# Reordering the mixers in front of an expert layer: projection columns, gated-attention levels and state-space heads in another order, host rows packed

## The chip, the cores and the metric

The kernel runs on one core of a Trainium2 chip. The metric is the device time of one execution in microseconds (us), the median of the runs. All tensors are float32. The engines are named as in the profile: PE (matmul), PEld (weight load), DVE (vector), ACT (scalar), POOL (GpSimd) and SP, whose queue issues the DMAs.

## The reference

One layer of a hybrid backbone over 256 context tokens and 256 latent tokens (D = 1024), then a mixture of experts over the latent tokens. Cut to what matters:

```python
hl = modulate(rmsnorm(xl, norm1_g), mod_l[0], mod_l[1])   # mod = silu(c) @ w_ada + b_ada
hc = modulate(rmsnorm(xc, norm1_g), mod_c[0], mod_c[1])
fl, fc = mixer_inputs(hl), mixer_inputs(hc)               # u = h @ w_in, split in three head groups
#   GLA:   q, k, v, gate, log decays through a low rank (16)      (chunked scan, both directions)
#   RWKV7: token shift of u; r, k, v, decay / a / gate through low ranks (matrix-valued decay)
#   SSD:   4-tap convolution + silu of xs, B, C; dt = softplus; z (8 heads, both directions)
(gla_c, gla_l), (rw_c, rw_l), (ssd_c, ssd_l) = token_mixers(fc, fl)
xl = xl + mod_l[2] * (concat(gla_out, rwkv_out, ssd_out) @ w_out)
hl = modulate(rmsnorm(xl, norm2_g), mod_l[3], mod_l[4])
xl = xl + mod_l[5] * moe(hl)                              # top 4 of 32 experts, clamped SwiGLU, 12 MB of weights each
return rmsnorm(xl, final_norm_g)
```

Context tokens only give the states from which the scans of the latent tokens start.

## The kernel before, in words

Every engine has one list of instructions, written out by hand, that it works off in order; `pe`, `dve`, `act`, `pool` and `sp` are their blocks. PSUM is handed round in four pairs of banks: `round_table()` lists for each product its pair and how many drains it gets. `R.claim` (PE) waits until all earlier products of that pair are drained, `R.filled` and `R.arrived` say that a product stands in it, `R.drained` and `R.emptied` that it has been read out. Nearly every matmul goes through the helper `mm` (L1786).

The stages, in PE's order:

1. Front. SP loads the identity, the tokens and the constants. ACT issues 22 small DMAs of bias, gain and shift rows into `prow`; PE transposes them (L1812, L1813) and DVE copies them into the column table `pc`. SP waits for those rows before it issues the first 8 tiles of `w_ada` (1 MB each, L549), and then 18 small DMAs of small matrices (L560). PE also transposes the latent tokens into `xT` (L1809). `modulation(n)` is one tile of the modulation (8 records of 128x512 on a quarter of the array each); from n = 4 on, filler matmuls stand between (L1798). Then come the normalized and modulated tokens `hT`.
2. Projections. `PROJ` lists 14 products of one or two column tiles of 128, over all 512 tokens or the 256 latent ones, each 8 matmuls deep: B, C, xs0, xs1, z0, z1 (state space), gq, gv, og, lg (GLA), rr, rk, rv, low (RWKV). `W_GROUPS` packs their columns into 7 loads. The other 16 modulation tiles stand between them (`ADA_AFTER`). DVE adds the taps of the convolutions and the token shifts (L1205).
3. Transposes and small sums: the tokens of xs, v, B by token, the log decays summed (`gs`, `gc`, `cc`), the state-space states `st` and scores `sc`.
4. State-space heads. `running_sums(h)` makes the cumulated decays of one head, DVE turns them into exponents (L1300), ACT takes exp (L891, L893), DVE multiplies the weights (L1312, L1320), PE forms the head's output `yp`. The low-rank products of RWKV (`rz`, `ra`, `rg`, `rkn`) and the GLA state `gS` are put between the heads.
5. GLA levels. The attention within 256 tokens is built from nine masked products `l0` to `l8`. For each of the eight levels after the first, POOL makes four exponent arguments (L674 to L677), ACT takes exp (L917), DVE multiplies them with the keys and queries (L1410, signalling `lk_ready`), PE forms two halves `a` and `b` of 8 small matmuls each, and DVE writes them into `att` under a mask (L1118, L1121). Two argument buffers take turns. Reciprocals of the state-space norm and of RWKV's keys (L1388, L1397) and POOL's RWKV preparation (L683 to L696) stand between the levels.
6. GLA output `go`, its norm (L1424), then `gla_done`.
7. RWKV: four tiles in two directions, a chain of small products (`squares`, `series`, ...); its first product `mix_matrices(0)` waits for `scale_by_decays` (L1448 to L1454).
8. Output projection, second norm, routing (L1606 to L1676).
9. Experts: 32 experts of 12 MB, streamed by SP through a ring of eight 2 MB buffers. SP issues the first ones after `cat_ready`, the end of stage 7 (L605).

Of the kernel before, what the change touches and what calls it, by code (L numbers as in the profile page):

```python
# [11 lines left out]
P = 128  # L12
# [55 lines left out]
class Rounds:  # L68
# [36 lines left out]
    def emptied(self, eng, name):  # L105
# [5 lines left out]
PROJ = [  # L111
    ("B", ((SSD0 + 1024, 128, False), (SSD0 + 1152, 128, False))),
    ("C", ((SSD0 + 1280, 128, True), (SSD0 + 1408, 128, True))),
    ("xs0", ((SSD0 + 512, 128, False), (SSD0 + 640, 128, False))),
    ("xs1", ((SSD0 + 768, 128, False), (SSD0 + 896, 128, False))),
    ("z0", ((SSD0, 128, True), (SSD0 + 128, 128, True))),
    ("z1", ((SSD0 + 256, 128, True), (SSD0 + 384, 128, True))),
    ("gq", ((0, 128, True), (128, 128, False))),
    ("gv", ((256, 128, False), (384, 128, False))),
    ("og", ((512, 128, True), (640, 128, True))),  # L120
    ("lg", ((768, 32, False),)),
    ("rr", ((RW0, 128, True), (RW0 + 128, 128, True))),
    ("rk", ((RW0 + 256, 128, False), (RW0 + 384, 128, False))),
    ("rv", ((RW0 + 512, 128, False), (RW0 + 640, 128, False))),
    ("low", ((RW0 + 768, 96, False), (RW0 + 864, 64, True))),
]

W_GROUPS = [(SSD0 + 1024, 512, ("B", "C")), (SSD0 + 512, 512, ("xs0", "xs1")), (SSD0, 512, ("z0", "z1")),
            (0, 512, ("gq", "gv")), (512, 288, ("og", "lg")), (RW0, 512, ("rr", "rk")), (RW0 + 512, 416, ("rv", "low"))]


ADA_AFTER = (1, 1, 1, 1, 2, 1, 1, 0, 2, 1, 2, 1, 1, 1)

RECIP_AT = 3
# [6 lines left out]
def round_table():  # L141
    t = [("x0", 0, 1), ("x1", 1, 1), ("prm", 2, 1), ("ada0", 3, 1), ("mt0", 0, 1)]
    t += [(f"h{i}", i % 2 + 2, 2) for i in range(4)]
    t += [("dtp", 0, 1), ("dt", 1, 1)]
    for i, (n, _) in enumerate(PROJ):
        t += [("gz", 0, 1)] if n == "rk" else []
        t.append((n, (i + 1) % 3, 1))
    for i in (1, 2):
        t += [(f"ada{i}", 3, 1), (f"mt{i}", 3, 1)]

    t += [("xst0", 0, 1), ("xst1", 1, 1), ("gs", 0, 1), ("gk", 1, 1), ("gvt", 0, 1), ("gc", 1, 1), ("Bt", 2, 1), ("cc", 3, 1), ("st", 0, 1), ("sc", 1, 1)]
    for q in range(4):
        t += [(n, g, 1) for n, g in ((("rz0", 1), ("rz1", 1)), (("ra", 0),), (("gS", 1), ("rg", 1)), (("rkn", 0),))[q]]
        t += [(f"dc{2 * q}", 2, 2), (f"dc{2 * q + 1}", 3, 2), (f"yp{q}", q % 2, 1)]
    t += [("sn", 2, 1)]

    for i in range(9):
        t += [(f"l{i}a", (2 * i) % 4, 1), (f"l{i}b", (2 * i + 1) % 4, 1)]
    t += [("rb", 0, 1), ("go", 2, 1), ("gn", 3, 1)]

    t += [("rvt", 1, 1)]
# [76 lines left out]
def hybrid_block(nc, a):  # L238

    with ExitStack() as ctx:  # L240
# [27 lines left out]
        pc = keep.take(162)  # L268
# [4 lines left out]
        dtw, rtw = keep.take(KD, 16), keep.take(KD, E)  # L273
        dtw_and_next = arena[:, dtw_at:dtw_at + KD * 16 + 16]
# [5 lines left out]
        muc, dall, dcol = keep.take(8), keep.take(8), keep.take(4)  # L280
# [22 lines left out]
        prow = sa.take(2, P)  # L303
        diagR = sa.take(4, P)
        sb_ = Area(scratch0, WORDS - 8192 + 4096)
        xtk, Btok = sb_.take(4, 512), sb_.take(2, 256)
# [3 lines left out]
        ea = sb_.take(16)  # L310
        xw = sb_.take(2, 2, 512)
        Sst = sb_.take(2, 512)
        scF, scB = sb_.take(2, 3, P), sb_.take(2, 3, P)
        eD, EI, CI, WD = sb_.take(2, 768), sb_.take(2, 512), sb_.take(2, 512), sb_.take(2, 768)
        ssq = sb_.take(4, L)
        gz = sb_.take(4, 256)
# [219 lines left out]
        def _(sp):  # L536
# [16 lines left out]
            for n in range(8):  # L553
                load_ada(n)
# [2056 lines left out]
```

## Time and profile before

| | us |
|---|---|
| runs shown | 1499.49, 1500.68, 1815.03; median 1500.68 |
| profiled execution | 1503.03, of which the span 1501.1 |
| PE busy | 1336.3 (89%) |
| DVE busy | 411.4 (27%) |
| ACT busy | 227.3 (15%) |
| POOL busy | 53.1 (4%) |
| DMA | 452.44 MB, mean 301 GB/s |
| mean granted TensorE clock | 0.957 of 2.4 GHz |

How to read it: an engine's busy share is an average over nine stages with different limits. Idle time of an engine matters only where it is the engine on which the others wait. The profiled execution is 2.35 us above the median of the runs.

### The profile page before, as it was taken

To read this page: it belongs to the slowest core of one execution; us is meant where nothing else is said; L and a number is where in the kernel's file an instruction comes from. 1 tells how busy PE (TensorE), PEld (TensorE's weight loads), DVE (VectorE), ACT (ScalarE), POOL (GpSimd) and SP (SyncE) were. 2 spreads that over 40 slices of the span, in tenths; PEclk is the share of its full clock that TensorE was granted. 3 is DMA by queue.
4 is the path that set the end of the run, shared out by engine and by line. 5 is a ranking of instruction groups with operands and counts; after the bars stand their busy time and mean duration, and the time that the engine had idled before them with its cause. 6 is when DMAs were issued, how large, how long until landed. Compare 5 with 4: busy or idle time off the path is not lost.

```text
span 1501.1 us, 21678 instructions
## 1 busy us (share of the span) xinstructions
PE 1336.3 (89%) x9148; PEld 639.8 (43%) x9148; DVE 411.4 (27%) x959; ACT 227.3 (15%) x426; POOL 53.1 (4%) x84
## 2 busy tenths in 40 slices
PE   4999998644888979999999999999999999998997
PEld 2545546423878874333333333333333333333332
DVE  0131135487454442112112112112112112111211
ACT  2122103332232131001001001001001001000101
POOL 0000000043121000000000000000000000000000
PEclk8999999866899979999999999999999999999999
DMA  8536510000101197999999999999999999999995
GB/s 331 189 138 226 202 68 0 1 0 19 40 3 59 47 380 290 424 428 426 427 426 428 428 427 428 427 428 427 427 427 429 428 427 427 428 428 426 428 426 234
DMA packets 44886, 452.44 MB, mean 301 GB/s; under 512 B 6998, under 2 KB 10036, under 8 KB 17044
## 3 DMA queue, kind: packets, MB, share of 16 engines
q1 hardware_dynamic: 44544, 451.38, 72.2%
q8 instruction: 53, 0.87, 0.2%
q10 hardware_dynamic: 276, 0.08, 0.0%
q14 instruction: 13, 0.11, 0.0%
HBM read 450.40 MB, written 1.05 MB: 301 GB/s over the span
## 4 chain that ended last, share of the span: by engine, by line
PE 43%; DMA 16%; DVE 3%; issue 1%; ACT 1%; DVEq 0%; SPq 0%
PE PS L1786 42%; DMA arena<-in_moe_w_gu 16%; PE PS L2499 1%; DVE arena L1708 1%; DVE arena L1711 1%; DVE arena L1714 1%; PE PS L2490 1%; ACT arena L1026 0%; DVE arena L1707 0%; DVE arena L1614 0%; ACT arena L1101 0%; DVE arena L1779 0%; ACT L1019 0%; DVEq L240 0%; DVE arena L1643 0%
## 5 line engine op out<-in xcount | busy, mean ns | idle before, releaser
L1786 PE MATMUL PS<-arena 128*64 128x512 f32 (+11 forms) x8746 | 1282.1, 425 | 113.5 <-DVE arena L1410 23.7
L1786 PEld LDWEIGHTS PS<-arena 128*64 128x64 f32 (+7 forms) x8746 | 593.2, 152 | 750.5 <-issue 599.9
L1707 DVE TENSOR_SCALAR arena<-PS 128x256 f32<-128x256 f32 x64 | 38.6, 602 | 522.3 <-PE PS L1786 522.3
L1052 ACT ACTIVATE arena<-arena 128x256 f32<-128x256 f32 x64 | 26.7, 418 | 491.1 <-DVE arena L1707 491.1
L1734 DVE TENSOR_TENSOR arena<-PS,arena 128x512 f32<-128x512 f32 x32 | 22.1, 692 | 219.3 <-PE PS L1786 219.3
L1062 ACT COPY arena<-PS 128x256 f32<-128x256 f32 x32 | 11.9, 373 | 288.7 <-PE PS L2490 288.7
L2499 PE MATMUL PS<-arena 128*128 128x128 f32 x128 | 26.2, 286 | 29.9 <-DVE arena L1714 29.9
L1205 DVE SCALAR_TENSOR_TENSOR arena<-PS,arena 128x255 f32<-128x255 f32 (+5 forms) x68 | 32.7, 481 | 41.8 <-ACT arena L820 39.5
L1708 DVE TENSOR_SCALAR arena<-PS 128x256 f32<-128x256 f32 x64 | 39.0, 610 | 0.0
L2499 PEld LDWEIGHTS PS<-arena 128*128 128x128 f32 x128 | 14.5, 141 | 56.1 <-DVE arena L1714 30.8
L1711 DVE SCALAR_TENSOR_TENSOR arena<-arena 128x256 f32<-128x256 f32 x64 | 27.3, 426 | 2.8
L1714 DVE TENSOR_TENSOR arena<-arena 128x256 f32<-128x256 f32 x64 | 27.3, 426 | 2.2
L1047 ACT COPY arena<-PS 128x512 f32<-128x512 f32 x32 | 18.8, 587 | 46.1 <-PE PS L1786 46.1
L1057 ACT COPY arena<-PS 128x256 f32<-128x256 f32 x64 | 23.5, 368 | 5.6 <-PE PS L2499 5.6
L1477 DVE TENSOR_TENSOR arena<-arena,PS 128x256 f32<-128x256 f32 x40 | 16.9, 421 | 24.4 <-PE PS L1786 23.7
L1690 DVE TENSOR_SCALAR arena<-arena 128x128 f32<-128x128 f32 x64 | 19.1, 341 | 0.0
L1463 DVE COPY arena<-PS 128x512 f32<-128x512 f32 x16 | 11.0, 689 | 27.6 <-PE PS L1786 27.6
L2490 PEld LDWEIGHTS PS<-arena 128*128 128x128 f32 x64 | 6.5, 141 | 24.3 <-issue 24.3
L983 ACT COPY arena<-PS 128x512 f32<-128x512 f32 x16 | 9.4, 587 | 41.3 <-PE PS L1786 41.3
L674 POOL TENSOR_TENSOR arena<-arena 128x128 f32<-128x128 f32 x8 | 3.5, 443 | 320.6 <-DVE arena L1328 309.6
L1300 DVE TENSOR_SCALAR arena<-PS,arena 128x256 f32<-128x256 f32 (+1 forms) x32 | 11.1, 410 | 11.3 <-ACT arena L891 11.2
L2490 PE MATMUL PS<-arena 128*128 128x128 f32 x64 | 14.0, 301 | 0.0
(276 smaller groups left out, 464.0 us busy)
## 6 DMA issues: line engine op xcount, KB each, us to landing
arena<-in_moe_w_gu SPq DMA_DIRECT2D x128, 2048.0 KB, 26.5
arena<-in_moe_w_down SPq DMA_DIRECT2D x64, 2048.0 KB, 29.0
arena<-in_w_ada SPq DMA_DIRECT2D x24, 1024.0 KB, 7.4
arena<-in_w_in SPq DMA_DIRECT2D x5, 2048.0 KB, 9.2
arena<-in_w_out SPq DMA_DIRECT2D x4, 1024.0 KB, 6.7
arena<-in_w_in SPq DMA_DIRECT2D x1, 1664.0 KB, 6.9
arena<-in_consts SPq DMA_DIRECT2D x1, 1536.0 KB, 11.0
arena<-in_w_in SPq DMA_DIRECT2D x1, 1152.0 KB, 5.6
```

The costliest lines, as they stand in the source:

```text
L1052: act.activation(sgm[:, 256 * half:256 * half + 256], glu[:, 256 * half:256 * half + 256], ACT.Sigmoid, scale=ALPHA).then_inc(sig_ready, 1)
L1057: act.copy(actT[:, 2 * half:2 * half + 2].rearrange("p a b c -> p (a b c)"), src).then_inc(actT_ready, 1)
L1205: ins = dve.scalar_tensor_tensor(out=d_, in0=s_, scalar=wgt, in1=d_, op0=ALU.mult, op1=ALU.add)
L1690: ins = dve.tensor_scalar(selw[:, i, :, :], slot_ids.unsqueeze(1).to_broadcast([P, 2, SLOTS]), pos(i), gates[:, i, bass.ds(e, 1)], ALU.is_ ...
L1707: dve.tensor_scalar(by_rest(glu), of_half(0), LIMIT, None, ALU.min).then_inc(glu_ready, 1)
L1708: dve.tensor_scalar(by_rest(lin), of_half(1), LIMIT, -LIMIT, ALU.min, ALU.max).then_inc(moe_vec, 1)
L1711: dve.scalar_tensor_tensor(out=lin[:, cols], in0=lin[:, cols], scalar=1.0, in1=glu[:, cols], op0=ALU.add, op1=ALU.mult).then_inc(moe_vec, 1)
L1714: dve.tensor_tensor(act_[:, cols], lin[:, cols], sgm[:, cols], ALU.mult).then_inc(act_ready, 1)
L1734: dve.tensor_tensor(ye, PS[:, 3, :], m5h, ALU.mult).then_inc(ye_ready, 1)
L1786: ins = pe.matmul(out, lhsT, rhs, start=start, stop=stop, skip_group_check=skip)
L2490: ins = pe.transpose(PS[:, 3, t * P:t * P + P], selw[:, t, :, :].rearrange("p a b -> p (a b)"), ident)
L2499: ins = pe.transpose(dst[:, c * P:c * P + P], act_[:, (2 * half + c) * P:(2 * half + c + 1) * P], ident)
```

## The change

The host lays the inputs out anew: all bias, gain and shift rows as one `params` table (128 x 170), the small matrices as one `mats` table, the tokens, `xT`, `w_ada`, `w_in` and `w_out` so that each load is one contiguous run per partition. The first eight tiles of `w_ada` come as four loads of 2 MB. ACT's row DMAs, the transposes into `prm` and `xT` and three memsets are gone. On SP's queue the order is params, identity, three double tiles of `w_ada`, tokens, the fourth, mats, constants.

The projections come in the order ll, gq, gv, og, B, C, xs0, xs1, z0, z1, rk, rr, sg, rv. `ll` is one tile of 128 columns that holds the RWKV low-rank columns (96) and the GLA ones (32), which were two tiles (`low` and `lg`). GLA's small products stand between gq and B, the levels l0 to l8 from B to rk, each in two halves with half a projection tile (4 matmuls) between them; a level is one PSUM product now, with one drain. PSUM has five groups: the last pair is shared by the modulation products, in bank 7. The state-space heads are formed in four pairs, with `rv`, `rz0`, `rz1`, `ra`, `rkn`, `rg` and `rvt` between. The state-space norm (`sn`) and `rb` go into the RWKV stage. `w_out` isn't held back until `gla_done`.

```diff
-            sp.wait_ge(rows_in, 16 * N_ROWS)
-            for n in range(8):
-                load_ada(n)
...
+            sp.dma_start(prm, a["params"]).then_inc(params_in, 16)
+            sp.dma_start(Cb(C_ID), a["consts"][:, 0:P]).then_inc(ident_in, 16)
+            for n in (0, 2, 4):
+                load_ada(n)
+            sp.dma_start(xtok, a["tokens"]).then_inc(x_in, 16)
+            load_ada(6)
+            sp.dma_start(mats, a["mats"]).then_inc(mats_in, 16)
...
+    t += [("ll", 0, 2), ("gq", 1, 1), ("gz", 2, 1), ("gv", 0, 1), ("gk", 2, 1), ("gs", 3, 1), ("og", 1, 1), ("gvt", 2, 1), ("gc", 3, 1)]
+    t += [("B", 0, 1), ("C", 1, 1), ("ada1", 4, 1), ("mt1", 4, 1), ("xs0", 0, 1), ("xs1", 1, 1), ("gS", 3, 1), ("z0", 0, 1), ("z1", 1, 1)]
+    t += [(f"l{i}", 2, 1) for i in range(9)]
...
@@ tensor
+            project_in("B", 1, early)
+            level(0, 1)
+            project_in("B", 1, late)
+            project_in("C", 0)
+            project_in("C", 1)
+            modulation_columns(1)
+            level(1, 0)
+            project_in("xs0", 0, early)
+            level(1, 1)
+            project_in("xs0", 0, late)
+            level(2, 0)
...
+            project_in("sg", 0)
...
+            running_sums(0)
+            pe.wait_ge(xw_ready, 4)
+            R.emptied(pe, "Bt")
+            R.claim(pe, "st")
...
+            project_in("rv", 0)
+            decay_logits(0)
+            running_sums(1)
+            R.emptied(pe, "st")
+            head_pair(0)
+            project_in("rv", 1)
+            decay_logits(1)
+            running_sums(2)
+            head_pair(1)
...
+            running_sums(3)
+            head_pair(2)
...
+            values_by_token("rvt")
+            head_pair(3)
@@ vector
+            level_out(dve, 1)
+            level_keys(2)
+            level_out(dve, 2)
+            level_keys(3)
+            convolve(2, "xs0")
+            level_out(dve, 3)
+            level_keys(4)
...
+            for q in range(4):
+                if q:
+                    dve.wait_ge(w_ready, 2 * q)
+                exponents(2 * q)
+                exponents(2 * q + 1)
+                if q:
+                    gather_heads(q - 1)
+                weights(2 * q)
+                weights(2 * q + 1)
...
+                if q == 1:
+                    shift("rv", 4, (vT[:, 0, :], P, NT), (vT[:, 1, :], P, NT))
...
+            dve.wait_ge(kk_std, 1)
+            for c in range(2):
+                dve.reciprocal(kk[:, c, :], kk[:, c, :]).then_inc(kk_norm, 1)
+            gather_heads(3)
...
@@ vector, RWKV stage
+                    if s == 0 and j == 0:
+                        ssd_scale()
+                    if s == 0 and j == 2:
+                        ssd_norm()
```

## Rows read from the trace of the kernel before

**Rows 1.** Busy time by stretch: stretch and its length, each engine's busy time, PEclk, DMA share, GB/s
```profile
19.98:39.67 19.69, 16.35 (x95) 6.04 (x95) 1.22 (x6) 3.40 (x6) 0.00 (x0) 0.74 0.94 377
56.35:226.80 170.45, 168.22 (x573) 84.81 (x573) 42.40 (x87) 23.11 (x30) 0.00 (x0) 0.98 0.41 149
226.80:241.16 14.36, 9.76 (x83) 9.01 (x79) 7.00 (x16) 7.49 (x11) 0.00 (x0) 0.91 0.00 1
241.16:320.00 78.84, 57.64 (x236) 37.99 (x236) 43.99 (x103) 26.40 (x31) 6.42 (x10) 0.85 0.00 1
320.00:355.00 35.00, 9.61 (x132) 7.29 (x128) 33.23 (x33) 5.99 (x9) 23.67 (x31) 0.55 0.00 1
355.00:372.96 17.96, 10.73 (x44) 6.19 (x44) 8.82 (x13) 5.97 (x10) 0.00 (x0) 0.88 0.03 3
372.96:521.00 148.04, 128.88 (x3322) 118.56 (x3323) 71.82 (x168) 35.64 (x80) 21.51 (x35) 0.94 0.09 33
565.80:1501.00 935.20, 881.83 (x4352) 322.07 (x4352) 174.94 (x448) 96.87 (x213) 0.00 (x0) 1.00 0.98 414
```
**Rows 2.** Timeline of the front: start, length, engine, line, operation [idle before, releaser]
```profile
14.86 4.09 SPq L549 DMA_DIRECT2D arena<-in_w_ada  x8
...
19.98 1.94 PE L1786 MATMUL PS<-arena 128*32 128x512 f32 x8 [4.73 <-DMA arena<-in_w_ada]
...
29.86 1.93 PE L1786 MATMUL PS<-arena 128*32 128x512 f32 x8 [0.56 <-DMA arena<-in_w_ada]
...
39.73 0.69 DVE L1161 COPY arena<-PS 128x512 f32<-128x512 f32 x1 [15.20 <-PE PS L1786]
```
**Rows 3.** PE's groups by form, 61.5 to 226.8 us: records, busy, mean ns of one
```profile
L1786 PE MATMUL PS<-arena 128*128 128x512 f32 x201 | 87.9, 595 | 0.0
L1786 PE MATMUL PS<-arena 128*128 128x256 f32 x176 | 41.2, 394 | 0.0
L1786 PE MATMUL PS<-arena 128*32 128x512 f32 x144 | 23.3, 601 | 2.2 <-DMA arena<-in_w_ada 2.2
```
**Rows 4.** DVE's groups by form, 56 to 373 us
```profile
L1121 DVE COPY_PREDICATED arena<-arena,PS 128x512 f32<-128x512 int32 x14 | 9.5, 730 | 0.1
...
L1300 DVE TENSOR_SCALAR arena<-PS,arena 128x256 f32<-128x256 f32 x16 | 7.6, 478 | 11.3 <-ACT arena L891 11.2
L1397 DVE RECIPROCAL arena<-arena 128x512 f32<-128x512 f32 x2 | 6.7, 3336 | 0.0
...
L1351 DVE TENSOR_TENSOR arena<-arena 128x1024 f32<-128x1024 f32 x1 | 1.2, 1226 | 0.0
```
**Rows 5.** ACT's and POOL's groups by form, up to 373 us
```profile
L891 ACT ACT_TABLE_LOAD x2 | 2.6, 1283 | 0.0
...
L690 POOL TENSOR_TENSOR arena<-arena 128x1024 f32<-128x1024 f32 x1 | 2.4, 2352 | 0.0
```
**Rows 6.** Timeline of DVE: the taps of one convolution; one tile of a shift
```profile
96.57 6.17 DVE L1205 SCALAR_TENSOR_TENSOR arena<-PS,arena 128x254 f32<-128x254 f32 x12 [12.30 <-ACT arena L820]
...
214.28 0.75 DVE L1251 TENSOR_SCALAR arena<-PS,arena 128x512 f32<-128x512 f32 x1 [9.25 <-PE PS L1786]
215.06 2.04 DVE L1205 SCALAR_TENSOR_TENSOR arena<-PS,arena 128x255 f32<-128x255 f32 x4
```
**Rows 7.** Timeline of the GLA levels
```profile
329.12 2.52 POOL L687 TENSOR_TENSOR arena<-arena 128x1024 f32<-128x1024 f32 x1
329.47 2.72 DVE L1410 TENSOR_TENSOR arena<-arena 128x512 f32<-128x512 f32 x1
...
336.61 0.63 DVE L1410 TENSOR_TENSOR arena<-arena 128x512 f32<-128x512 f32 x1
...
337.29 1.26 PE L1786 MATMUL PS<-arena 32*128 32x128 f32 x16 [3.79 <-DVE arena L1410]
```
**Rows 8.** Timeline of the first RWKV products
```profile
372.96 1.13 PE L1786 MATMUL PS<-arena 64*64 64x64 f32 x32 [4.83 <-DVE arena L1454]
...
383.13 0.69 DVE L1463 COPY arena<-PS 128x512 f32<-128x512 f32 x1 [5.04 <-PE PS L1786]
```

More of the change, by code:

```diff
@@ L485, in Cb @@
             return C[:, i:i + n, :].rearrange("p a b -> p (a b)")
[L488 removed]
+        loads = [(s, 2, "ada", 2 * m) for m, s in enumerate((0, 2, 4, 12))]
         def streamed(kind, n):
@@ L509, in hybrid_block @@
                 holder[q] = (s, base[s])
+        for n in range(0, 8, 2):
+            place["ada", n + 1] = place["ada", n]
         def w_in_tile(n):
@@ new lines, in _ @@
+            dve.wait_ge(gn_std, 1)
+            run(dve.reciprocal(gsq, gsq))
+            for q in range(2):
+                step(dve.scalar_tensor_tensor(out=gO[:, q, :], in0=gO[:, q, :], scalar=B(72 + q), in1=gsq[:, q, :], op0=ALU.mult, op1=ALU.mult))
+            settle()
+            R.emptied(dve, "og")
+            dve.tensor_tensor(cat[:, 0:2, :], gO, gog, ALU.mult).then_inc(gla_done, 1)
+            shift("rr", 0, (rT[:, 0, :], P, L), (rT[:, 1, :], P, L))
+            shift("sg", 7, (sgT, 64, L))
@@ L1432, in _, with ssd_scale, ssd_norm @@
+            def ssd_scale():
+                dve.wait_ge(sn_std, 1)
+                run(dve.reciprocal(s2[:, 0:512], s2[:, 512:1024]))
+            def ssd_norm():
+                for q in range(4):
+                    step(dve.scalar_tensor_tensor(out=cat[:, 4 + q, :], in0=cat[:, 4 + q, :], scalar=B(68 + q),
+                                                  in1=s2[:, q // 2 * 256:q // 2 * 256 + 256], op0=ALU.mult, op1=ALU.mult))
             dve.wait_ge(rw_pre, 1)
@@ L1949, in _ @@
             R.filled("gc", ins)
-            modulation_columns(2)
+            project_in("B", 0)
+            level(0, 0)
+            project_in("B", 1, early)
[9 more added lines that the diff above has]
+            level(2, 0)
+            project_in("xs0", 1, early)
+            level(2, 1)
+            project_in("xs0", 1, late)
+            level(3, 0)
+            project_in("xs1", 0, early)
+            level(3, 1)
+            project_in("xs1", 0, late)
+            level(4, 0)
+            project_in("xs1", 1, early)
+            level(4, 1)
+            project_in("xs1", 1, late)
+            level(5, 0)
+            pe.wait_ge(gkw_ready, 1)
+            R.emptied(pe, "gvt")
+            R.claim(pe, "gS")
+            for d in range(2):
+                for t in range(2):
+                    ins = mm(pair("gS")[:, 256 * d:256 * d + 256], gkw[:, t, P * d:P * d + P], gvk[:, t, :], start=t == 0, stop=t == 1)
+            R.filled("gS", ins)
+            level(5, 1)
+            project_in("z0", 0)
+            project_in("z0", 1)
+            level(6, 0)
+            project_in("z1", 0)
+            level(6, 1)
+            project_in("z1", 1)
+            level(7, 0)
+            pe.wait_ge(conv_silu, 2)
             R.claim(pe, "Bt")
@@ L1955, in _ @@
             R.filled("Bt", ins)
+            level(7, 1)
+            R.claim(pe, "sc")
+            for g in range(2):
+                for t in range(2):
+                    ins = mm(pair("sc")[:, 512 * g + 256 * t:512 * g + 256 * t + 256], BT[:, g, L + t * P:L + t * P + P], CT[:, g, :])
+            R.filled("sc", ins)
+            project_in("rk", 0, early)
+            level(8, 0)
+            project_in("rk", 0, late)
+            level(8, 1)
             pe.wait_ge(dt_ready, 1)
```

983 lines of the change are left out of this document (470 added, 513 removed).

## The prediction, made before the changed kernel was run

> **What bounds the kernel now.** I read the busy time by stretch first, because 89% busy PE hides stages with different limits. The experts fill 935 us: PE is busy for 882 us of it and the DMA queues for 98%, at 414 GB/s [rows 1]. Their first load waits for the end of the RWKV stage, and neither their bytes nor their code change, so this stretch moves as a block and the question is only how much earlier it starts. In the projections PE is busy for 168.2 of 170.5 us at full clock, so PE alone bounds them; DVE works a quarter of that time [rows 1]. From 241 to 320 us, the state-space heads, no engine is full: PE 57.6, DVE 44.0, ACT 26.4 of 78.8 us. From 320 to 355 us, the levels, PE does 9.6 us of work in 35 us, at a mean clock of 0.55, behind a DVE that is busy for 33.2 us. Until 373 us the GLA norm adds 18 us with PE 60% busy. So 146 us between the projections and the first RWKV product hold only about 88 us of PE work, part of it at the low clock, while 128 us of DVE time lie idle under the projections. That is the reserve that the change draws on.
>
> **The change part by part.** All times are in the profiled execution (span 1501.1, with its surroundings 1503.0), 2.35 us above the median.
>
> *Front.* Now the first modulation tile starts at 19.98 us, because SP issues it at 14.86, after the rows; the tiles then land one per 2.5 us (19.98 and 29.86 are four tiles apart), and the eighth one's product is read at 39.73 [rows 2]. The new queue carries 10.7 MB up to the last of the eight tiles: 0.15 for params and identity, 8.4 for the tiles, 2.1 for the tokens. At 2.5 us per MB (1.05 MB a tile, 420 GB/s) this is 25.5 us, and with 2.6 us from issue to flow (5.1 us from 14.86 to 19.98 less one tile) the last lands at 28 to 29. Two tiles of 1 to 1.9 us and one row of fillers later the product is read at about 32.7: 7 us gained. Bounds: 2 us, if the mix of sizes flows at the 377 GB/s of the stretch and PE comes back to its low clock [rows 1], and 10 us.
>
> *One tile fewer.* A full tile is 16 records of 128x512, 87.9/201 = 0.437 us each, so 7.0 us, half of that for a latent tile [rows 3]. `ll` saves one: 7.0 us, PE-bound time, no unknown. The transposes into `xT` and `prm` lay in the DMA wait and save nothing more. Fifteen full tiles become fourteen.
>
> *From the first projection to the last before rv.* Twelve full tiles 83, twelve half tiles 41, 16 modulation tiles (23.3 us less the 6.9 of lg, over 16: about 1.05) 17, gz, gk, gs, gvt, gc, gS, Bt, sc, cc, go, gn, xst and the modulation's transposes about 21 (their records at 0.11 us per 128 columns at the full clock), nine levels of 0.8 (1.26 at a low clock [rows 7], 0.63 were it all at the full one) 7: 169 us of PE work. Is a level ready when PE comes to it? Between two levels PE has at least 7 us of projection. A level needs four small POOL operations (1.9 us), an exp, one DVE multiply of 0.63 and a masked copy of 1.35 [rows 4, 7]; the convolution of a pair of tiles, 6.2 us [rows 6], comes in between three times, each after the key product that the next level needs. DVE's sum per full tile is 2.0 plus 3.1, of 7.0 us. I follow the queues level by level and find one stall, 0.5 us, where the modulation row is copied after B's convolution. Then `st` cannot be claimed until DVE has shifted `sg`, behind a reciprocal of 3.35 [rows 4], the GLA product and the shift of rr: PE has run 170 us and waits till 177 after its start, with one running sum to fill it. Sum 177 us. Zero stalls is the lower bound; the upper one is 20 us, eight levels that each wait 2.5 us for a chain such as now costs PE 3.79 us [rows 7].
>
> *Heads.* After st (3.4 us) DVE is the engine to follow. Its work in 241 to 320 was 44.0 us [rows 1]; about 9.5 of that (scores, GLA keys and state, gate, squares, norm, last gather) goes elsewhere, and the shift of rv comes in, two tiles of 0.75 and 2.04 [rows 6]: 40 us. Waits that stay: the rz1 product behind rv, and before the last pair ACT's three sigmoids with two table loads of 1.28 [rows 5], 6 us together. With st 3.4 that is 49 us. The same DVE work took 60 us in the old lock step, in which each head's exponents waited for ACT (11.3 us [rows 4]); in pairs, the second head's exponents cover the first one's exp.
>
> *From the last weights to the first RWKV product.* Two reciprocals 6.7 [rows 4]; POOL's two products 2.35 each [rows 5] and DVE's two of 1.23 [rows 4] in the same time; ssd variance 0.7 and the first scaling 1.7. DVE's multiply took 2.72 instead of 0.63 us when it began inside a POOL operation and ended with it [rows 7], so the four products run one after the other: 7.2. Sum 16.5 us. POOL's preparation of RWKV's keys, three operations of about 2.4, now lies beside the last heads instead of the levels. The row shows one DVE operation held for 2.1 us, so I allow 3 us for all of it. The Trainium skill (SBUF — State Buffer, "SBUF: two separate sides") states more and speaks against the change: DVE, with two SBUF inputs, and POOL exclude each other for a whole instruction, and the loser blocks. By that rule all 7 us of the preparation could be lost to DVE and the sum would be 4 us longer; the row agrees in kind.
>
> *RWKV stage.* It gains the norm's reciprocal (3.35) between the first squares' copy, at 383.13 [rows 8], and the series that PE waits for, 2 us of four scalings, and `rb` (1 us) in the chain at its end: 5 us, bounds 2 and 9. `w_out` and `xT` load earlier, in idle DMA time, and cost nothing; were that cover gone, 5.2 MB at 414 GB/s would be 13 us, but the output projection is 130 us away.
>
> *The sum.* From the start of the projections to the RWKV product: 177 + 49 + 16.5 = 242.5, against 372.96 - 56.35 = 316.6: 74 us less (the saved tile is in it). The front gives 7, the RWKV stage takes 5, POOL's lock and some thirty hand-overs of about 0.1 us take 6. 74 + 7 - 5 - 6 = 70: 1503 - 70 = 1433, and 1431 as a median.
>
> **The clock** is the second place. PE at 0.55 in the levels and 1.00 in the projections [rows 1] means that the same 128x512 record costs 0.87 or 0.44 us. In the levels PE had waited about 4 us before each burst; under the projections it has no such wait, so I price all of it at 2.4 GHz. The Trainium skill (TensorE: Matmul & The Clock Gate, Part 1) says that the half clock is the default and that activity releases it. By that rule too the result hangs on PE having no holes, and holes would turn it round: that is the slower rival.
>
> **Rivals.**
> - *The lock step stays* (17%). Each queue works in order, so a level can stand behind a convolution and a head behind the rv shift. Against it: DVE has 28% of slack under the projections. For it: `st` waits for `sg` already. Price: the heads at their old pace, 60 + 6 + 3.4 for 49, is +20, and eight levels that wait 1.3 us each, +10: 1461.
> - *Only the front and the tile pay* (8%). With so many products in few PSUM groups, some thirty claims could each wait 2 us for a drain on a DVE with 5 us operations in front. Then 60 us are given back and the result is 1491, within 2%. The present projections claim in the same way and wait 2.2 us in all [rows 3], which speaks against it.
> - *PE falls to 1.2 GHz in the projections* (4%), slower. Place: the 155 us of projection and modulation matmuls, where each level is now a point at which PE may wait. Price: all of them at 1.2 GHz is +155, 1586; it decides from 100 us on, two thirds of that stretch. Against it: 0.98 in this stretch, with the DMA wait of 2.2 us inside [rows 1, 3].
> - *The packed rows do nothing* (in the front's bound): the bytes are the same, and if these and not the issue at 14.86 set the end, the front gives 2 and the total 1436.
>
> **How the numbers follow.** Main case 71%: 1431, own range 1415 to 1450 (front 5, RWKV 4, no stalls and no lock -6 below; 8 for the lock, 10 for stalls above). The range of 8 in 10 takes in the lock step and ends at 1464. A measurement can tell about 2% from no change, 30 us here: faster than 1471 in the first two cases, 0.88; within 2%, 0.08; slower 0.04.
>
> **What would show it.** In the profile after: the first modulation product at 8 to 10 us; `ll` starting near 49; PE near 100% and PEclk 1.0 from there to about 220, no idle before a level over 1 us, an idle of up to 4 us before st; the heads' four pairs 8 to 14 us apart, DVE over 80% busy; the first 64x64 product of RWKV at 292 to 299; the experts' stretch unchanged at 935 us, 70 us earlier. Wrong would be: PE waiting at levels for DVE, a clock under 0.9 in the projections, or experts that end less early than they begin.

## The result and the profile after

The changed kernel takes 1436.56 us (median of four runs, 1436.17 to 1439.66), the one before 1502.78 in the same series: ratio 0.9577, 95% interval 0.9556 to 0.9597, so 4.2% faster. One of the four executions of the kernel before, 1815.03 us, was a slow one and stands outside the ratio; the three others have a median of 1500.68. The forecast was 1431, range 1414 to 1464. The profiled execution has a span of 1434.4 us against 1501.1. Below, stages are compared between profiled executions, one for each kernel.

Busy time by stretch after the change, columns as in [rows 1]: stretch and its length, PE, weight loads, DVE, ACT, POOL, PEclk, DMA share, GB/s.

```profile
29.52:35.46 5.94, 5.94 (x27) 2.75 (x28) 1.05 (x5) 0.90 (x2) 0.00 (x0) 0.55 1.03 432
50.54:235.78 185.24, 180.33 (x813) 101.78 (x813) 71.95 (x141) 44.71 (x58) 13.81 (x32) 1.00 0.38 138
235.78:289.93 54.15, 48.34 (x197) 29.70 (x197) 41.63 (x90) 19.59 (x24) 7.65 (x4) 0.95 0.11 39
289.93:310.45 20.52, 11.15 (x40) 7.91 (x41) 16.89 (x16) 5.08 (x10) 9.44 (x5) 0.73 0.00 1
310.45:454.00 143.55, 127.91 (x3318) 116.47 (x3319) 75.97 (x171) 37.01 (x81) 21.29 (x34) 0.95 0.05 18
499.00:1434.40 935.40, 881.71 (x4352) 321.80 (x4352) 175.66 (x450) 96.86 (x213) 0.00 (x0) 1.00 0.98 414
```

The levels' stretch at clock 0.55 is gone. The projections, now with the levels inside, have PE busy for 97% at full clock. (PEclk 1.00 is 2.4 GHz, 0.50 is 1.2 GHz.) The experts take 935.4 us as before. In the heads PE is now busier than DVE (48.3 against 41.6 of 54.2 us).

The timeline of the changed kernel, PE, then DVE from the heads on. The end of a line names the idle time before it and what ended it.

```profile
10.10 3.64 PE L1782 MATMUL PS<-arena 128*32 128x512 f32 x16 [10.10 <-DMA arena<-in_ada_first]
...
29.52 1.93 PE L1782 MATMUL PS<-arena 128*32 128x512 f32 x8 [3.41 <-DMA arena<-in_ada_first]
31.38 2.50 PE L1794 MATMUL PS<-arena 128*128 128x128 f32 x10
33.82 1.57 PE L1782 MATMUL PS<-arena 128*32 128x512 f32 x8
...
235.78 47.31 PE L1782 MATMUL PS<-arena 128*128 128x256 f32 x188 [3.92 <-DVE arena L1186]
...
289.93 7.75 PE L1782 MATMUL PS<-arena 128*64 128x256 f32 x32 [5.82 <-DVE arena L1354]
305.08 3.40 PE L1782 MATMUL PS<-arena 128*128 128x256 f32 x8 [7.40 <-DVE arena L1401]
310.45 0.69 PE L1782 MATMUL PS<-arena 64*64 64x64 f32 x32 [1.98 <-issue]
```
```profile
241.26 1.23 DVE L1327 COPY arena<-PS 128x1024 f32<-128x1024 f32 x1 [5.63 <-PE PS L1782]
...
265.44 1.22 DVE L1377 TENSOR_TENSOR arena<-PS,arena 128x1024 f32<-128x1024 f32 x1 [4.50 <-PE PS L1782]
...
286.29 3.49 DVE L1354 SCALAR_TENSOR_TENSOR arena<-arena 128x256 f32<-128x256 f32 x4
...
291.62 6.55 DVE L1395 RECIPROCAL arena<-arena 128x512 f32<-128x512 f32 x2
298.10 0.38 DVE L1362 SCALAR_TENSOR_TENSOR arena<-arena,PS 128x256 f32<-128x256 f32 x1
298.51 3.23 DVE L1400 TENSOR_TENSOR arena<-arena 128x1024 f32<-128x1024 f32 x1
301.78 3.25 DVE L1401 TENSOR_TENSOR arena<-arena 128x1024 f32<-128x1024 f32 x1
```

The two rows of 3.23 and 3.25 us and the one of 3.49 us are DVE operations beside POOL's. PE waits at no level; its only hole over 1 us between the first projection and the heads is 3.92 before `st` (235.78). In the heads each engine waits for the other in turn: DVE for `st` (5.63) and for the second decay product `rz1` (4.50), PE for the last pair's weights (5.82), and then for the gate's squares (7.40). Behind the wait before `st`, PE's clock is low for 3.4 us, although the stage's mean is 0.95:

```profile
236.30:239.70 3.40, 3.40 (x10) 2.69 (x9) 0.00 (x0) 0.00 (x0) 0.00 (x0) 0.50 0.00 0
```

Where the 66.7 us came from, stage by stage:

| stage | before | after | gained | forecast |
|---|---|---|---|---|
| to the first projection | 56.35 | 51.6 | 4.7 | 7 |
| first projection to `st` | | 184.2 | | 177 |
| `st` to the reciprocals | | 55.8 | | 49 |
| reciprocals to first RWKV product | | 18.8 | | 16.5 |
| the three together | 316.6 | 258.8 | 57.8 | 74, less 6 for lock and hand-overs |
| first RWKV product to the norm behind the output projection | 174.6 | 171.3 | 3.3 | -5 |
| the rest | 953.5 | 952.6 | 0.9 | 0 |

### The profile page after: what moved, and what is told of

The parts are those of the page before. It is cut to its first block, busy times and chain, and to the rows that moved or that the text cites. A ratio compares the mean times of both kernels' runs of the same rounds, so it can differ in the third digit from the quotient of the medians.

```text
span 1434.4 us, 21531 instructions
## 1 busy us (share of the span) xinstructions
PE 1315.4 (92%) x9114; PEld 628.4 (44%) x9114; DVE 410.8 (29%) x957; ACT 227.5 (16%) x426; POOL 53.4 (4%) x81
## 4 chain that ended last, share of the span: by engine, by line
PE 45%; DMA 17%; DVE 3%; issue 1%; ACT 1%; DVEq 0%; SPq 0%
PE PS L1782 43%; DMA arena<-in_moe_w_gu 17%; PE PS L2546 1%; DVE arena L1704 1%; DVE arena L1710 1%; DVE arena L1707 1%; PE PS L2537 1%; PE PS L2435 0%; ACT arena L1008 0%; DVE arena L1703 0%; DVE arena L1610 0%; ACT arena L1083 0%; DVE arena L1775 0%; ACT L1001 0%; DVEq L262 0%
## 5 line engine op out<-in xcount | busy, mean ns | idle before, releaser
L1782 PE MATMUL PS<-arena 128*64 128x512 f32 (+10 forms) x8730 | 1265.2, 421 | 79.2 <-DMA arena<-in_ada_first 17.7
L1782 PEld LDWEIGHTS PS<-arena 128*64 128x64 f32 (+5 forms) x8730 | 585.6, 150 | 704.5 <-issue 604.4
L1029 ACT COPY arena<-PS 128x512 f32<-128x512 f32 x32 | 18.8, 587 | 45.1 <-PE PS L1782 45.1
L1101 DVE COPY_PREDICATED arena<-arena,PS 128x512 f32<-128x512 int32 x14 | 9.5, 733 | 32.7 <-PE PS L1782 32.7
L1680 DVE TENSOR_SCALAR arena<-arena 128x64 f32<-128x64 f32 x64 | 12.2, 252 | 6.7 <-PE PS L1782 6.4
```

The costliest lines, as they stand in the source:

```text
L1782: ins = pe.matmul(out, lhsT, rhs, start=start, stop=stop, skip_group_check=skip)
```

## The experiments

All are made from the changed kernel. Medians of one kernel in different series differ by up to 3 us (the kernel before: 1501.09 to 1504.01), and the read of dt (the state-space step sizes) alone, which ends the same front in all but e12, comes at 49.96 to 51.81 us. By their ratios to the kernel before, e6, e7, e8 and e11 can't be told from the changed kernel, the intervals of e2 and e5 touch its own, e1, e3 and e4 are slower, e9, e10 and e12 faster. So I judge effects below 5 us by the length of a stage. "From dt" counts from that read: in the changed kernel `st` is at 184.2 from dt, the reciprocals at 240.0, the first RWKV product at 258.8.

These figures have a scatter of their own. In eight of the twelve traces with the changed kernel's order of projections (e2, e5 to e10 and e12) the granted clock falls to 0.50 for 3.4 us in the projections, although PE has no hole there, right behind 24 products of 8 columns (`cc`). In the changed kernel, e3, e4 and e11 it doesn't. e2 first, then the changed kernel:

```profile
203.00:206.40 3.40, 3.40 (x7) 1.72 (x7) 0.33 (x2) 0.20 (x1) 0.00 (x0) 0.50 0.00 0
```
```profile
203.00:206.40 3.40, 3.40 (x18) 2.24 (x18) 0.32 (x2) 0.20 (x1) 0.00 (x0) 1.00 0.00 0
```

Where `st` keeps its wait, it then comes 185.6 to 186.2 us behind dt, against 183.8 to 184.2 without the low clock and without added work. A difference of 2 us from dt therefore need not be the edit's.

**e1: the levels behind the projections.**

```diff
             project_in("B", 0)
-            level(0, 0)
-            project_in("B", 1, early)
-            level(0, 1)
-            project_in("B", 1, late)
+            project_in("B", 1)
...
             project_in("z1", 1)
-            level(7, 0)
+            for i in range(9):
+                level(i, 0)
+                level(i, 1)
```

> The nine levels stand in one run behind the last z1 tile; all state-space tiles, their convolutions and the GLA state come before them. Same instructions, another order. My account (the gain of the levels lies in their cover by projections): 34 us of level chain, nine at 3.8 us each as before the change, stand alone, while the 12.8 us of level products leave the projections: +21 us, and some us more where PE falls to the low clock, so 1456 to 1463 us against 1436.6. Rival (PE has the same work in any order and DVE catches up, the gain came from elsewhere): at most +5 us, 1442. In the trace the first account shows PE idle about 2 to 3 us before each level at a granted clock under 0.8.

Measured 1462.19 us (1460.89 to 1463.35), ratio 0.9731 (0.9715 to 0.9747); `st` at 207.0 from dt, 22.8 later. A stretch of its trace with eight levels by busy time, and two of them in the timeline:

```profile
181.00:212.00 31.00, 19.12 (x131) 14.82 (x132) 13.76 (x22) 2.52 (x4) 6.43 (x16) 0.53 0.16 67
```
```profile
188.80 2.50 PE L1771 MATMUL PS<-arena 32*128 32x128 f32 x16 [1.54 <-DVE arena L1099]
192.85 2.51 PE L1771 MATMUL PS<-arena 32*128 32x128 f32 x16 [1.55 <-DVE arena L1099]
```

A level costs 4.05 us in a run of levels, 1.54 of them idle (2 to 3 had been expected) and the rest at the low clock. Placed between tiles it costs its 1.42 us of PE time (12.8 us for nine) and no wait. Placing them so is worth 23 us against one run of levels within the new kernel; the rival account (at most 5 us) is out.

**e2: lock step within a pair of heads.**

```diff
                 exponents(2 * q)
-                exponents(2 * q + 1)
                 if q:
                     gather_heads(q - 1)
                 weights(2 * q)
+                exponents(2 * q + 1)
                 weights(2 * q + 1)
```

> Only the order on DVE within a pair of state-space heads: exponents, weights, exponents, weights in place of exponents twice, weights twice. If DVE bounds all of the heads (the forecast): 8 heads that wait 1.4 us each for ACT, as the 11.3 us before the change, +11 us: 1448 us. If PE bounds the first two pairs and DVE only the last two: about half, +5 us: 1441. If the waits lie in the idle time of DVE (9 us in this stretch): 1437.

Measured 1444.04 us (1442.55 to 1445.45); from `st` to the reciprocals 60.55 us for 55.84, that is +4.7, and the first RWKV product 7.0 later from dt, of which 1.9 lie ahead of `st`, where the edit changes nothing (the low clock above). DVE's waits for ACT, by line:

```profile
L1337 DVE TENSOR_SCALAR arena<-PS,arena 128x256 f32<-128x256 f32 x16 | 7.6, 478 | 1.9 <-ACT arena L883 1.9
L1346 DVE TENSOR_TENSOR arena<-arena 128x512 f32<-128x512 f32 x8 | 5.5, 693 | 5.7 <-ACT arena L887 3.6 <-ACT arena L885 2.0
```

The lock step makes DVE wait 5.7 us ahead of the weights, where the changed kernel waits 0.0, but only 4.7 us arrive at the end of the heads. By the stage that is the middle account: up to `rz1`, where DVE had waited 4.50 us for PE, it now waits 2.15, so PE bounds that part and hides the first pairs' share of the waits. The measured time, 1444, lies between the middle account (1441) and the full one (1448).

**e3, e4, e5, e11: 16 records more of PE work, at four places.** e3 multiplies the second `gv` tile twice, e4 the second `rv` tile, e5 makes the product for `ra` five times, e11 the one for `rkn`. The edits of e3 and e5 (e4 and e11 have the other name in the same place):

```diff
+                if (name, j) == ("gv", 1):
+                    for k in ks:
+                        mm(pair(name)[0:m, 512 * j:512 * j + n], wt[:, k, col:col + m], hT[:, k, NT - n:NT], start=k == 0, stop=k == 7)
...
             R.claim(pe, "ra")
-            for c in range(2):
+            for c in 5 * (0, 1):
```

> The second gv tile is multiplied twice: 16 records of 128x512 more, 7.0 us of PE work, in the projections. If PE alone bounds them: +7.0 us from the first projection to st, 191 us instead of 184, and 1443.6. If something else (DVE's chain, the loads) had slack to give and bounds a part: the 4.9 us in which PE idles there take some of it up, +2 us: 1438.7.

Measured 1444.52 us (1443.57 to 1446.54); `st` at 190.8 from dt for 184.2: +6.6, nothing absorbed. PE alone bounds the projections.

> The second rv tile is multiplied twice: 8 more 128x512 products, 16 records of 0.437 us, 7.0 us of PE work in the heads before the second decay product. If PE bounds the heads up to there: +7 us, 1443.6. If DVE bounds them, as the forecast had it, the 5.8 us that PE idles before the last pair take it up: +1.2 us, 1437.8.

Measured 1445.02 us (1442.04 to 1446.78); first RWKV product at 265.65 from dt, +6.8. DVE's wait at `rz1` grew from 4.50 to 11.38 us, and the one of PE before the last pair stayed at 5.82:

```profile
270.45 1.23 DVE L1377 TENSOR_TENSOR arena<-PS,arena 128x1024 f32<-128x1024 f32 x1 [11.38 <-PE PS L1782]
...
294.93 8.06 PE L1782 MATMUL PS<-arena 128*64 128x256 f32 x32 [5.82 <-DVE arena L1354]
```

So PE bounds the heads up to `rz1`, against the forecast's "DVE is the engine to follow": PE's idle of 5.8 us lies behind that point and can't take up what comes ahead of it.

> The product for ra is made five times: 7.0 us of PE work more (16 records of 128x512), behind the second pair of heads. If DVE bounds the heads from the second decay product on: PE's idle of 5.8 us before the last pair takes most of it up, +1.2 us: 1437.8. If PE bounds the heads to their end: +7 us, 1443.6.

Measured 1445.5 us (1441.57 to 1448.73; the profiled execution is the slowest of the four), and the first RWKV product 12 us later from dt, 10.3 of them in the heads: both accounts were wrong, since 16 records took about 13 us and not 7. Two things were mixed in it, the place and the clock, so I ran the next one.

> The product for rkn is made five times, 16 records of 128x512 more on all 128 rows, at about the place where e5 had 16 more on 32 rows, which ran at 0.91 us each and at a granted clock of 0.75. If the clock fell there because PE was kept busy without a break: it falls here too and PE works 14 us more. If it fell because of the products on 32 rows: 0.44 us each, 7.0 us more PE work at clock 1.00, and the time is 1440 to 1444 instead of 1446.

Measured 1440.68 us (1435.22 to 1440.97); first RWKV product at 261.5 from dt, +2.7 us. PE's records of these shapes in 17 us of either trace, 266 to 283 in e5, then 268 to 285 in e11 (records, busy us, mean ns of one):

```profile
L1782 PE MATMUL PS<-arena 32*128 32x512 f32 x17 | 12.2, 890 | 0.0
```
```profile
L1782 PE MATMUL PS<-arena 128*128 128x512 f32 x20 | 8.9, 597 | 0.0
...
L1782 PE MATMUL PS<-arena 32*128 32x512 f32 x4 | 2.0, 613 | 0.0
```

And the busy time by stretch, e5 first, with the stretch in which its clock is low, then e11:

```profile
266.00:283.00 17.00, 17.00 (x54) 8.92 (x53) 12.66 (x30) 6.28 (x7) 0.00 (x0) 0.75 0.28 116
...
274.40:291.40 17.00, 17.00 (x24) 6.94 (x23) 5.87 (x15) 6.89 (x7) 0.94 (x2) 0.50 0.00 0
```
```profile
266.00:283.00 17.00, 17.00 (x66) 9.54 (x65) 13.21 (x31) 8.71 (x10) 1.11 (x2) 1.00 0.24 102
```

PE is busy for all of 17 us in both, yet the granted clock is 0.75 with the products on 32 rows and 1.00 with those on 128. That is one trace of each. With the clock out of the way (e11), 4.3 of the 7.0 us vanish in PE's idle time before the last pair, which is 1.5 us then: behind `rz1` DVE bounds most of the heads. The rest comes through DVE's wait of 3.43 for `rkn`, which stands behind the extra products in PE's queue.

**e6: another PSUM pair for st.**

```diff
-    t += [("st", 1, 1), ("rv", 0, 1),
+    t += [("st", 3, 1), ("rv", 0, 1),
```

> Only the PSUM pair of st is another one: the pair of gn and the heads' outputs, not the one of sg. If PE's 3.9 us of idle before st are the wait for the drain of sg: they go, st starts right behind the last projection, and with PE as the bound of the first heads all later stages come 3.9 us earlier: 1432.7. If DVE is the engine to follow there (it copies st only behind the shift of sg): the gain is lost again in the wait for DVE, 0 to 1 us: 1436.

Measured 1435.43 us (1432.35 to 1436.22), ratio 0.955 (0.9533 to 0.9567), not to be told from the changed kernel's 0.9577 by the runs. In the trace the idle before `st` is gone, and `rz1` and the reciprocals come 3.9 us earlier from dt (236.1 for 240.0). That it is just the length of the wait is chance. The low clock behind the wait is gone too:

```profile
232.40:240.00 7.60, 7.60 (x28) 4.88 (x27) 7.35 (x17) 3.21 (x4) 0.00 (x0) 1.00 0.00 0
```

That gives 1.7 us more, and e6 has the low clock in the projections, which takes about as much. Against e8, which has it too, the first RWKV product comes 5.8 us earlier (255.3 for 261.1). Then the RWKV stage is 174.9 instead of 171.3 us long: 1.0 us is lost in its first 15 us, where the clock is low for 10.1 us instead of 6.8, the rest about 100 us on, where this trace has gaps that no wait explains. e8 and the table behind it show these.

**e7: the gate behind the first RWKV scaling.** The product with the gate, the squares and the norm's product go behind the first scaling, `sn` to another pair.

```diff
-            run(dve.tensor_tensor(cat[:, 4:8, :], cat[:, 4:8, :], sz, ALU.mult))
-            dve.tensor_tensor(ssq, cat[:, 4:8, :], cat[:, 4:8, :], ALU.mult).then_inc(ssq_ready, 1)
...
             scale_by_decays(0)
+            run(dve.tensor_tensor(cat[:, 4:8, :], cat[:, 4:8, :], sz, ALU.mult))
+            dve.tensor_tensor(ssq, cat[:, 4:8, :], cat[:, 4:8, :], ALU.mult).then_inc(ssq_ready, 1)
```

> The gate product, the squares and the norm's product of the state-space heads move from ahead of the first RWKV product to behind it (sn in another PSUM pair); the last gather stays. My account: reciprocals to 298.2, gather 0.5, POOL's two products one behind the other to 303.4, scaling 1.3, so the first RWKV product 5.5 us earlier, and DVE's 3 us of moved work lie beside PE's matrices in the RWKV stage, of which 0 to 2 come back: 1431 to 1433. Rival: the moved work stands in the RWKV chain in full, 1434.6.

Measured 1437.53 us (1433.63 to 1439.23). From the reciprocals to the first RWKV product it took 12.96 us for 18.83, the 5.9 expected; but from there to PE's first transposes 10.35 us instead of 4.52. The moved 3 us stood in the chain of the first matrices, on DVE, and PE waited for it, 3.12 us where it had waited 1.18; and the norm's product, moved too, took PE from 314.6 to 318.2, between the matrices and the transposes. The next 24 us made 2.5 of that good; the whole stage is 175.4 us for 171.3. Both accounts were too kind.

**e8: the norm left out of the RWKV stage.**

```diff
-                    if s == 0 and j == 0:
-                        ssd_scale()
-                    if s == 0 and j == 2:
-                        ssd_norm()
```

> Leaves out the reciprocal (3.34 us) and the four scalings (about 2 us) of the state-space norm in the RWKV stage, so its output lacks that factor. The forecast priced this work at 4 to 5 us of the stage: then 1432. If it lies in DVE's idle time there, as the stage's 142.9 us after against 146.2 before suggest: 0 to 1 us, 1436.

Measured 1439.63 us (1438.58 to 1440.22). The stage, from its first product to the norm behind the output projection, in the changed kernel and in e8:

```profile
310.45:481.78 171.33, 149.29 (x3438) 135.41 (x3439) 91.14 (x204) 46.99 (x98) 22.02 (x35) 0.95 0.20 80
```
```profile
311.89:484.08 172.19, 148.38 (x3438) 134.25 (x3439) 86.23 (x199) 46.99 (x98) 21.84 (x35) 0.96 0.20 80
```

4.9 us less DVE work, and the stage is not shorter: the forecast's 4 to 5 us for this work were 0. Nor is it hidden by the scatter of the stage: the same record that comes 46.7 us behind the first product in the changed kernel, with the norm done, comes 47.1 us behind it in e8. What varies between the traces is the time that PE spends in gaps that the trace gives to "issue", that is, to no wait it shows, and the time at the low clock:

| | before | after | e1 | e2 | e3 | e4 | e5 | e6 | e7 | e8 | e9 | e10 | e11 | e12 |
|---|---|---|---|---|---|---|---|---|---|---|---|---|---|---|
| stage, us | 174.6 | 171.3 | 172.9 | 173.0 | 171.9 | 171.6 | 172.4 | 174.9 | 175.4 | 172.2 | 174.0 | 172.2 | 172.7 | 177.6 |
| issue gaps, us | 5.5 | 1.3 | 2.7 | 1.2 | 3.7 | 3.4 | 3.8 | 4.4 | 2.6 | 3.3 | 3.6 | 1.6 | 4.4 | 6.3 |
| low clock, us | 21.0 | 16.8 | 15.0 | 19.4 | 17.2 | 16.8 | 14.1 | 17.9 | 15.0 | 13.9 | 16.2 | 10.6 | 14.1 | 11.0 |

The longest stage has the largest sum of gaps, but the two go together only loosely: e4 has 2.1 us more of them than the changed kernel and is 0.3 us longer. e2's length lies rather in the clock, and e7's in what the edit moved. Here are three of the kernel before, then the largest of the changed one:

```profile
449.36 7.42 PE L1786 MATMUL PS<-arena 64*64 64x64 f32 x251 [1.36 <-issue]
459.38 1.08 PE L1786 MATMUL PS<-arena 64*64 64x64 f32 x29 [2.60 <-issue]
480.45 4.76 PE L1786 MATMUL PS<-arena 64*64 64x64 f32 x155 [1.28 <-issue]
```
```profile
414.84 4.92 PE L1782 MATMUL PS<-arena 64*64 64x64 f32 x154 [0.49 <-issue]
```

Over the eight traces in which this stage's code is the same (after, e1 to e6 and e11) it takes 171.3 to 174.9 us, and the changed kernel's is the shortest. So the 3.3 us that this stage gave in the profiled run are within what it varies by, and e6's missing gain is too. The Trainium skill (Runtime: NRT & Kernel Launch, Instruction fetch mechanics) describes engines that fetch their program in blocks through a DMA queue, and calls the cost mostly hidden. No run here shows that the gaps are such fetches.

**e9, e10, e12: what the account is good for.** e9 puts the head pairs ahead of the second `rv` tile and the second decay product on PE, and on DVE the reciprocals right behind the last weights, with the shift of `rv` beside POOL's two products; the transposes `rvt` go behind the heads, and `st` is as in e6. e10 also spreads the gate, squares and norm over the first two series of RWKV. e12 adds ten idle products in the front and puts `rg` behind the last pair.

```diff
             head_pair(0)
-            project_in("rv", 1)
-            decay_logits(1)
-            running_sums(2)
-            head_pair(1)
             R.claim(pe, "ra")
...
+            running_sums(2)
             pe.wait_ge(kk_sq, 1)
             R.claim(pe, "rkn")
...
+            head_pair(1)
             running_sums(3)
             head_pair(2)
+            project_in("rv", 1)
+            decay_logits(1)
...
             for c in range(2):
                 dve.reciprocal(kk[:, c, :], kk[:, c, :]).then_inc(kk_norm, 1)
+            decay_bias(1)
...
+            shift("rv", 4, (vT[:, 0, :], P, NT), (vT[:, 1, :], P, NT), between=decay_scale)
             gather_heads(3)
```

> Same work in another order, with st in the other PSUM pair: on PE the running sums, the products for ra and rkn and the head pairs go ahead of the second rv tile and the second decay product, which now fill PE's wait for the last pair's weights; on DVE the two reciprocals stand right behind the last weights, then the second decay bias and the shift of rv, beside POOL's two products. My account (PE and DVE bound the heads in turn, each waiting for the other: 3.9 us before st, 4.5 us at the second decay product, 5.8 us before the last pair, 4.8 us for POOL's products): the first RWKV product comes about 12 us earlier after the read of dt than the 258.8 us of the changed kernel, at 247, and the time is 1425. Rival (one engine is full there, DVE with the shift of rv behind the reciprocals): only st's wait goes, 255 us and 1433.

Measured 1426.57 us (1422.8 to 1427.47), ratio 0.9483 (0.9462 to 0.9505); first RWKV product at 247.7 from dt, as the first account had it.

> The kernel of the reordered heads, and the gate product, squares, norm product and norm of the state-space heads spread over the first two series of the RWKV stage, where DVE has idle time; e7 had put them into the chain of its first matrices and lost there what it had gained ahead of them. My account: 5 us less than the reordered heads alone before the first RWKV product, none given back: 1420. Rival: the RWKV stage is longer by what was moved in: 1425.

Measured 1422.82 us (1422.1 to 1425.38), ratio 0.9471 (0.9453 to 0.949): 14 us below the changed kernel, the intervals apart. From e9 the runs can't tell it (the intervals overlap); in the traces the first RWKV product comes 3.9 us earlier, at 243.8 from dt. Its heads by busy time, its POOL products, and DVE beside them:

```profile
235.00:299.00 64.00, 55.49 (x321) 34.19 (x320) 57.45 (x114) 24.68 (x33) 19.79 (x17) 0.95 0.09 33
```
```profile
282.46 2.36 POOL L695 TENSOR_TENSOR arena<-arena 128x1024 f32<-128x1024 f32 x1 [17.58 <-DVE arena L1399]
284.90 2.35 POOL L696 TENSOR_TENSOR arena<-arena 128x1024 f32<-128x1024 f32 x1
...
284.09 2.04 DVE L1188 SCALAR_TENSOR_TENSOR arena<-PS,arena 128x255 f32<-128x255 f32 x4
286.16 2.18 DVE L1405 TENSOR_SCALAR arena<-arena 128x2048 f32<-128x2048 f32 x1
```

DVE is busy for 90% of this stretch, PE for 87%: there is little left in it. The whole stage is 172.2 us for e9's 174.0, but the moved work isn't free. PE waits longer for the same transposes, e9 first, then e10:

```profile
329.25 1.09 PE L2200 MATMUL PS<-arena 128*128 128x128 f32 x8 [0.38 <-DVE arena L1501]
```
```profile
325.08 1.97 PE L2204 MATMUL PS<-arena 128*128 128x128 f32 x8 [3.77 <-DVE arena L1497]
```

An earlier wait of 2.25 us is 0.18 instead, and the record that comes 46.7 us behind the first product in e9 comes 48.8 us behind it in e10. So about 2 of the 3.9 us are given back there, although e10's clock is low for 3.4 us less up to that record; e7 gave back 3.3 of 5.9. Fewer issue gaps later on cover it in this trace.

> The kernel of e10 with two small edits. Ten more idle products on PE between the third and the fourth pair of the first modulation tiles, 2.8 us of the 3.4 to 5.0 us that PE waits there for the load: if PE then stays at the upper clock, the last products and the idle products between them take 3.5 us instead of 6.0, and dt is read up to 2.5 us earlier, at 48 to 49 us; rival, the load ends this stretch and the clock doesn't matter: 50 us. And rg's product goes behind the last pair of heads, which in e10 waited 4.1 us behind rg for the second decay bias: if DVE, full from 270 to 291 us, sets the first RWKV product, that gives nothing there. Together 1420 to 1422, against 1422.8 of e10.

Measured 1423.8 us (1422.4 to 1424.27), ratio 0.9484 (0.9464 to 0.9504), as e10. The front gained as expected, dt is read at 48.40 instead of 50.30, and the first RWKV product came at 290.92 for 294.08; then the stage took 177.6 us, with the largest issue gaps of all, so the time missed the expected 1420 to 1422. `rg`'s place gave about 1 us, where nothing had been expected.

## Why the prediction was right, and where its errors met

The sign, the mechanism and the size of the main term held: DVE's level chain is free under the projections (e1, e3), the pairs save part of ACT's waits (e2), and the experts moved as a block. The forecast missed the gain between the profiled executions by only 3.3 us (70 against 66.7; the medians, 1431 and 1436.56, by 5.6) because terms wrong by 8 to 10 us each cancelled, and that is luck. One of its own signs failed: the first RWKV product was to come at 292 to 299 us and came at 310.45.

- *Front, forecast 7, measured 4.7* (4.5 to 6.4 with the spread of dt's read). The last pair of tiles was used at 29.52, a little later than the 28 to 29 named, and PE, after 3.41 us of waiting, did its last 6 us at clock 0.55. It is the return to the low clock that the lower bound spoke of, and e12 takes 1.9 us of it back with idle products.
- *Projections and levels, forecast 169 us of PE work in 177, measured 180 in 184.* The step that failed first is "nine levels of 0.8". I took it from the level at 337.29 in [rows 7], 1.26 us at clock 0.50. The same 16 records at the same clock take 2.50 us in e1. In the kernel before, the two halves of a level have a PSUM pair each and no wait between them; the change gives a level one pair and makes the second half, on the other 64 rows, wait for the first. The first tenth of a microsecond of a level shows it, the kernel before first, then e1: four records (32 rows each) have begun, or two.

```profile
337.29 0.61 PE L1786 MATMUL PS<-arena 32*128 32x128 f32 x4 [3.79 <-DVE arena L1410]
```
```profile
188.80 0.58 PE L1771 MATMUL PS<-arena 32*128 32x128 f32 x2 [1.54 <-DVE arena L1099]
```

The nine levels' PE work is 12.8 us, 5.8 more than priced. The Trainium skill (TensorE: Matmul & The Clock Gate, Part 3) says that products on distinct row groups run at the same time; the rows agree with it, and the diff showed the added wait. The rest of the 11 us is mostly in the tiles. A latent tile was priced at half a full one, 3.5 us, where [rows 3] has 41.2/176 = 0.234 us a record, 3.75 a tile; and the twelve full ones, 83 in the forecast, took about 87 (194 records, 87.8 us). The wait before `st` came out as written, 3.92 us, and e6 names it.
- *Heads, forecast 49, measured 55.8.* "DVE is the engine to follow" failed for the first two pairs: the forecast had the wrong engine there. I had summed DVE's 40 us (41.6 measured) and never PE's, which is 48.3: with the rv tiles (14 us) moved in, PE is the fuller one up to `rz1` (e4), DVE behind it (e11). Of the 48.3, about 1.7 (half of 3.4) are the low clock behind the wait before `st`; the forecast had priced that wait, and not the clock after it. "DVE over 80% busy" was 77%.
- *To the first RWKV product, forecast 16.5, measured 18.8.* Reciprocals, lock and order came as written: 6.55, and four products that end one after the other, from 298.3 to 305.0. Missing was the norm's product on PE, 3.40 us at the low clock after 7.40 of idle. The variance and the scaling behind it, priced at 2.4, took 1.9. (Row 329.47 in [rows 7] doesn't end with the POOL operation, as the forecast reads it, but 0.55 us behind it; the term stands either way.) The lock in the heads, allowed 3 us, is the row at 286.29: 3.49 for 1.40, 2.1 us once. The longer time that the Trainium skill's rule (SBUF — State Buffer, "SBUF: two separate sides") would give, all 7 us of POOL's preparation, did not come: only its last operation met a DVE operation with two SBUF inputs. Taken operation by operation the traces agree with the rule, here and in e10, where DVE's operations with an input in PSUM ran beside POOL's products at their usual 2.04 us.
- *RWKV stage, forecast +5, measured -3.3.* The norm costs nothing there (e8), and the 3.3 are within the stage's scatter. That is luck: the term was wrong by 8 us and made good most of the three stages' 10. The stage was priced as if each DVE microsecond in it stood in the chain; but DVE is idle for 80 of its 171 us, enough to hold 5 of work. `rb`, 1 us of the term, was not tested alone.
- *Lock and hand-overs, forecast 6:* 2.1 were the lock; no other wait at a hand-over is seen in the projections.

The rivals: the lock step was priced at 20 us for the heads and 10 for waits at the levels; made on purpose within the pairs, it costs 4.7 in the heads (e2), and levels with nothing between them 23 (e1). Neither came. Thirty claims that each wait for a drain did not come either: only the one before `st` waited over 1 us. The front gave 4.7 us, not the 2 of packed rows that do nothing. PE at 1.2 GHz in the projections did not come (1.00), apart from the 3.4 us that eight of the later traces show.

What stays open: whether e1's low clock comes from the 1.5 us holes or from products on 32 rows, since it has both; why the clock falls behind `cc` in some traces and not in others; and what the issue gaps are. No run takes the packed rows or `ll` back alone, so their shares are read from the stages.

## What to carry to other kernels

Sum every engine for a stage, not the one that looks like its bound, and cut the stage where one engine waits for the other: here PE bounds up to one product and DVE behind it, and only an edit on the right side of that point pays. When work is moved to hide it, put it where its engine has a hole in the trace, not merely off the path it left: the same 3 us gave back 3.3 of the 5.9 us gained in e7 and about 2 of 3.9 in e10. Compare at one record early in a stage, not only at its end, where other scatter has come in. And read a row's conditions with its duration: a product's time held for four row groups in flight, and the change made it two. Price the clock behind a wait together with the wait.

## What the hardware showed that I had not expected

- *A busy PE can still lose its clock.* In e5, PE had had no hole for 39 us, and its records on 32 of the 128 rows followed each other every 0.43 us, when the clock fell to 0.50 at the seventh of 20 in a row. From then on one took 0.85 us, and the clock came back at 291.4, 5 us after the last of them. In e11, with four records on 32 rows and 20 on 128 at the same place, it stayed at 1.00. The levels between tiles, also on 32 rows, kept 1.00, and the sums `cc`, 24 products of 8 columns right behind the last level, were followed by 3.4 us at 0.50 in eight traces of twelve. What sets the fall off behind `cc` was not tested. The Trainium skill (TensorE: Matmul & The Clock Gate, Part 1) ties the clock to how busy PE is; by that e5 should have kept it, and the measurement decides.
- *POOL's hold on DVE goes by operation.* A multiply of two SBUF tensors beside POOL took 3.23 and 3.25 us, against 1.23 in [rows 4] alone; a scaling of one SBUF tensor took 2.18 when it began inside a POOL operation in e10, against 1.22 in the changed kernel, where it began 0.4 us before POOL's.
- *Issue gaps of 1.2 to 6.3 us in sum*, in a stage of some 3,400 short products and different from kernel to kernel, are as large as the effects one hunts there.
